# Output projection, both layer normalizations and the feed-forward part in one block

## The chip, the cores and the metric

The kernel runs on one core of one Trainium2 chip. The metric is the device time of one execution in microseconds; the time before is the median of three runs. A core has five instruction streams that run side by side and wait for each other by semaphores: TensorE (PE), VectorE (DVE), ScalarE (ACT), GpSimd (POOL) and SyncE (SP), which here only issues transfers.

## The reference, cut to what matters

Two layers of a decoder trunk over 1040 tokens (16 learned ones ahead of 1024), width 1024. Each layer mixes tokens in two branches, projects, normalizes, runs a gated feed-forward part with a causal convolution of width 3, and normalizes again.

```python
h = _layer_norm(concat(meta, x), ln_in_g, ln_in_b)
for l in range(DEPTH):                       # DEPTH = 2
    p = h @ w_in[l]
    ...                                      # two branches, gates -> mixed
    h = _layer_norm(DEEPNORM_ALPHA * h + mixed @ w_out[l], ln1_g[l], ln1_b[l])
    f = _conv_ffn(h, w_up[l], conv_w[l], conv_b[l], w_down[l])
    h = _layer_norm(DEEPNORM_ALPHA * h + f, ln2_g[l], ln2_b[l])
return h[:, N_META:]
```

`_layer_norm` takes mean and variance over the 1024 channels of a token: `(x - mu) * rsqrt(var + 1e-5) * g + b`. Everything is float32.

## The kernel before, in words

**Layout.** Activations lie transposed: channels on the 128 partitions, tokens along the free dimension (TP = 1044, in NB = 3 pieces of 348). The stream `h` is eight tiles (KD = 8) of 128 x 1044. For precision each operand of a large product is split into a high part, which fp32r holds, and the low rest (`h_hi`, `h_lo`; `w_hi`, `w_lo`), and `product` (lines 187 to 197) sums three passes, hi x hi, lo x hi and hi x lo: for a 128-column unit of weights 8 x 3 x 3 = 72 matmuls into one of two groups of three PSUM banks (`pset[0]`, `pset[1]`).

**Weights.** Each unit of weights takes one of two slots: SP loads it into `w_raw` (`load_unit`), GpSimd makes `w_hi` and `w_lo` from it (`split_unit`, lines 225 and 227), TensorE uses it. A slot of `w_raw` is free again when it is split, a slot of `w_hi` and `w_lo` when its product is done.

**Phases.** `Phase` opens a block with its own semaphores and programs for the engines, and ends in a barrier over all engines (line 121), after which no engine has work in flight. The two layers are one hardware loop over `layer(l)`. Around the change the phases are:

- The opening (lines 285 to 416): loads the tokens, normalizes them by token in three groups of chunks, transposes them, and makes `h_hi` (ScalarE) and `h_lo` (GpSimd, line 393) through four staging buffers. It also collects the per-channel vectors and stores them to DRAM at its end.
- The input projection's first phase (lines 497 to 614): five units of `w_in` are loaded, split and multiplied; ScalarE begins with issuing twelve transfers of other weights and tables.
- The output projection (lines 2027 to 2065): eight units of `w_out`; VectorE reads each product out as `r` (ALPHA * h_hi + product) and `l` (+ ALPHA * h_lo) into `acc`, eight float32 tiles.
- `layer_norm` (lines 2070 to 2119), a phase of its own. TensorE multiplies a matrix of ones with all eight tiles of `acc` for the mean (24 fp32 matmuls, two records each); VectorE subtracts it (`c0` to `c7`); ScalarE squares, TensorE sums the squares in the same way; ScalarE makes the reciprocal root (`ln`, `rs`); then for each tile VectorE scales (`n`), ScalarE adds the bias and writes `h_hi` (`hi`), VectorE writes `h_lo` (`lo`), and only then starts the next tile:

```python
for k in range(KD):
    dves.did(stt(acc[:, k, :], acc[:, k, :], vecs[:, g_col + k:g_col + k + 1], lrs[:, :], ALU.mult, ALU.mult), f"n{k}")
    low(k)
```

- The feed-forward part (lines 2148 to 2360): the 22 channel tiles are taken in 11 groups of two, alternately called A and B. Four up products of a group, then eight down products of the group before it, whose results VectorE adds to `acc` (`d0` to `d7`, line 2314). ScalarE and VectorE do the convolution, the SiLU and the gating between. At its start ScalarE and VectorE rebuild `acc` = ALPHA * (h_hi + h_lo) (lines 2261 and 2302).
- `layer_norm` again, then the next layer, or `final_output`, which adds `h_hi` and `h_lo` (line 431), transposes and stores.

The order on each engine is written out by hand; every named step adds one to its engine's semaphore, and others wait for that count.

Of the kernel before, what the change touches and what calls it, by code (L numbers as in the profile page):

```python
# [15 lines left out]
F32 = mybir.dt.float32  # L16
# [108 lines left out]
def build(nc, a, out):  # L125
# [61 lines left out]
    def product(bank, kt, lhs_hi, lhs_lo, rhs_hi, rhs_lo):  # L187

        last = None
        for k in range(kt):  # L190
            passes = ((lhs_hi, rhs_hi), (lhs_hi, rhs_lo), (lhs_lo, rhs_hi))
# [59 lines left out]

    cursor[0] = base
# [21 lines left out]
    for g, chunks in enumerate(in_groups):  # L274
# [6 lines left out]
        for k in range(KD):  # L281
            act_names += [f"aff{g}_{k}", f"hi{g}_{k}"]
            pool_names.append(f"lo{g}_{k}")
    dve_names += [f"row{n}_{i}" for n in range(DEPTH) for i in range(3)]
    with Phase(nc, "const_loaded", "inv_loaded", "act_steps", "dve_steps", "pool_steps", "pe_tr", "pe_rows", "rows_loaded", "vecs_out",
               *[f"tok{i}_loaded" for i in range(NC)]) as (block, sm):
        const_loaded, inv_loaded, act_s, dve_s, pool_s, pe_tr, pe_rows, rows_loaded, vecs_out = sm[0:9]
        tok_loaded = sm[9:]
# [4 lines left out]
        def _(sp):  # L293
# [93 lines left out]
        def _(pool):  # L387
            pools.give(pool)
            for g, chunks in enumerate(in_groups):
                c0, n = chunks[0], len(chunks)  # L390
                for k in range(KD):
                    pool.wait_ge(acts.sem, acts.of(0, f"hi{g}_{k}"))
                    pools.did(nc.gpsimd.tensor_tensor(h_lo[:, k, c0 * CH:(c0 + n) * CH], hst[(g * KD + k) % 4][:, 0:n * CH],
                                                      h_hi[:, k, c0 * CH:(c0 + n) * CH], ALU.subtract), f"lo{g}_{k}")

# [71 lines left out]
    def layer(l):  # L467
# [29 lines left out]
        with Phase(nc, "raw0_loaded", "raw1_loaded", "hi_done", "split", "used", "act_steps", "dve_steps", "pe_tile",  # L497
# [13 lines left out]
            totals = [1, 1, 2, 2, 2 + len(mix)]  # L511

            @block.sync
            def _(sp):
                split.give(sp)
                for u in range(5):
                    load_unit(sp, u, u % 2, loaded, split, units[u])
                    if u == 1:
                        sp.dma_start(vecs[:, :], vecs_d[l]).then_inc(vecs_in, 16)
# [6 lines left out]
            def _(pool):  # L526
                used.give(pool)
                for u in range(5):
# [1497 lines left out]
        acc = place("acc", [P, KD, TP], F32, TOP)  # L2026
        with Phase(nc, "raw0_loaded", "raw1_loaded", "hi_done", "split", "used", "dve_steps") as (block, sm):
            loaded, hi_done, split, used = stream(sm[0:5])
            dves = Steps(sm[5], ["r0", "l0", "r1", "l1"])
            w_out_v = a["w_out"][l].rearrange("(k p) n -> p k n", p=P)  # L2030

            @block.sync
            def _(sp):
                split.give(sp)
                with sp.Fori(0, KD // 2) as i:
                    for s in range(2):
                        load_unit(sp, i * 2 + s, s, loaded, split, [(kview(KD), w_out_v[:, :, ds(i * (2 * P) + s * P, P)])])

            @block.gpsimd
            def _(pool):  # L2040
                used.give(pool)
                with pool.Fori(0, KD // 2) as i:
                    for s in range(2):
                        split_unit(pool, i * 2 + s, s, i + 1, loaded, hi_done, split, (used.sem, used.of(i * 2 + (s - 1))))

            @block.tensor
            def _(pe):
                with pe.Fori(0, KD // 2) as i:
                    for s in range(2):
                        pe.wait_ge(split.sem, split.of(i * 2 + (s + 1)))  # L2050
                        pe.wait_ge(dves.sem, dves.of(i, f"r{s}", 1))
                        product(pset[s], KD, wtile(w_hi[s], KD), wtile(w_lo[s], KD), hk(m_hi), hk(m_lo)).then_inc(used.sem, 1)

            @block.vector
            def _(dve):
                dves.give(dve)
                stt = nc.vector.scalar_tensor_tensor
                with dve.Fori(0, KD // 2) as i:
                    for s in range(2):
                        def at(tile):  # L2060
                            return tile[:, ds(i * 2 + s, 1), :].rearrange("p o t -> p (o t)")
                        dve.wait_ge(used.sem, used.of(i * 2 + (s + 1)))
                        dves.did(stt(chunks3(at(acc)), chunks3(at(h_hi)), ALPHA, pset[s], ALU.mult, ALU.add), f"r{s}")
                        dve.wait_ge(dves.sem, dves.of(i, f"r{s}"))
                        dves.did(stt(at(acc), at(h_lo), ALPHA, at(acc), ALU.mult, ALU.add), f"l{s}")

        def layer_norm(g_col, b_col):  # L2070
            cursor[0] = base
            sq2 = [after(f"ln_sq{i}", [P, TP]) for i in range(2)]
            lrs = after("ln_rs", [P, TP])
            with Phase(nc, "pe_steps", "act_steps", "dve_steps") as (block, sm):
                pes = Steps(sm[0], ["mean"] + [f"v{k}" for k in range(KD)])
                acts = Steps(sm[1], [f"sq{k}" for k in range(KD)] + ["ln", "rs"] + [f"hi{k}" for k in range(KD)])
                dves = Steps(sm[2], [f"c{k}" for k in range(KD)] + [f"{n}{k}" for k in range(KD) for n in ("n", "lo")])

                @block.tensor
                def _(pe):  # L2080
                    pes.did(product32(pset[0], [(ones[:, :], acc[:, k, :]) for k in range(KD)]), "mean")
                    for k in range(KD):
                        pe.wait_ge(acts.sem, acts.of(0, f"sq{k}"))
                        for n in range(NB):
                            last = nc.tensor.matmul(pset[1][:, n, :], ones[:, :], sq2[k % 2][:, nrange(n)], start=(k == 0), stop=(k == KD - 1))
                        pes.did(last, f"v{k}")

                @block.scalar
                def _(act):
                    acts.give(act)  # L2090
                    for k in range(KD):
                        act.wait_ge(dves.sem, dves.of(0, f"c{k}"))
                        if k >= 2:
                            act.wait_ge(pes.sem, pes.of(0, f"v{k - 2}"))
                        acts.did(nc.scalar.activation(sq2[k % 2][:, :], acc[:, k, :], ACT.Square), f"sq{k}")
                    act.wait_ge(pes.sem, pes.of(0, f"v{KD - 1}"))
                    acts.did(nc.scalar.activation(chunks3(lrs[:, :]), pset[1], ACT.Ln, bias=EPS_LN, scale=1.0 / DM), "ln")
                    act.wait_ge(acts.sem, acts.of(0, "ln"))
                    acts.did(nc.scalar.activation(lrs[:, :], lrs[:, :], ACT.Exp, scale=-0.5), "rs")
# [316 lines left out]
```

## Time and profile before

| | us |
|---|---|
| median of 3 runs | 4536.91 (4532.87 to 4538.57) |
| the profiled execution | 4534.88 |
| its span, first to last instruction | 4533.1 |
| mean granted clock of TensorE, share of full | 0.932 |
| TensorE busy | 3877.1 (86%) |
| VectorE busy | 2027.8 (45%) |
| ScalarE busy | 1066.1 (24%) |
| GpSimd busy | 936.5 (21%) |

Busy times are sums over the span; engines overlap. In the rows further down a time at the start of a line is counted from the span's first instruction, the second number is the duration, and the bracket at the end says how long the engine had been idle and what released it.

### The profile page before, as it was taken

To read this page: it belongs to the slowest core of one execution; us is meant where nothing else is said; L and a number is where in the kernel's file an instruction comes from. 1 tells how busy PE (TensorE), PEld (TensorE's weight loads), DVE (VectorE), ACT (ScalarE), POOL (GpSimd) and SP (SyncE) were. 2 spreads that over 40 slices of the span, in tenths; PEclk is the share of its full clock that TensorE was granted. 3 is DMA by queue.
4 is the path that set the end of the run, shared out by engine and by line. 5 is a ranking of instruction groups with operands and counts; after the bars stand their busy time and mean duration, and the time that the engine had idled before them with its cause. 6 is when DMAs were issued, how large, how long until landed. Compare 5 with 4: busy or idle time off the path is not lost. (4 is left out here: it accounts for less than half of the span.)

```text
span 4533.1 us, 68171 instructions
## 1 busy us (share of the span) xinstructions
PE 3877.1 (86%) x28391; PEld 3522.9 (78%) x28391; DVE 2027.8 (45%) x2448; ACT 1066.1 (24%) x1504; POOL 936.5 (21%) x464
## 2 busy tenths in 40 slices
PE   3978889898795899999868889898968679999995
PEld 3655888886685899999754569797858579999993
DVE  2145346564415454454422434575633354445454
ACT  3245124222103111121222531341210121212112
POOL 3000320000231333333110014000013133333330
PEclk9988999999898999999978889998988889999997
DMA  4221236421310111111024112553222011111110
GB/s 100 70 68 29 80 110 188 121 70 59 112 32 28 43 47 43 47 47 43 14 63 105 48 34 84 162 163 85 65 98 80 5 47 47 43 47 43 47 38 37
DMA packets 370423, 305.20 MB, mean 67 GB/s; under 512 B 118167, under 2 KB 323571, under 8 KB 370147
## 3 DMA queue, kind: packets, MB, share of 16 engines
q1 hardware_dynamic: 331588, 243.02, 19.0%
q10 hardware_dynamic: 38559, 58.12, 3.7%
q8 instruction: 220, 3.60, 0.3%
q14 instruction: 56, 0.46, 0.0%
HBM read 218.82 MB, written 82.26 MB: 66 GB/s over the span
## 5 line engine op out<-in xcount | busy, mean ns | idle before, releaser
L225 POOL TENSOR_TENSOR w_hi<-w_raw,consts 128x1024 fp32r<-128x1024 f32 (+1 forms) x218 | 392.9, 1802 | 3410.7 <-PE psum L194 1226.1
L194 PE MATMUL psum<-h_hi,w_hi 128*128 128x348 f32 x3792 | 822.7, 326 | 222.1 <-POOL w_lo L227 182.2
L194 PEld LDWEIGHTS psum<-h_hi,w_hi 128*128 128x128 f32 x3792 | 644.9, 190 | 231.3 <-POOL w_lo L227 184.5
L194 PE MATMUL psum<-h_lo,w_hi 128*128 128x348 f32 x3792 | 813.8, 323 | 0.0
L194 PE MATMUL psum<-h_hi,w_lo 128*128 128x348 f32 x3792 | 811.2, 322 | 0.0
L194 PEld LDWEIGHTS psum<-h_lo,w_hi 128*128 128x128 f32 x3792 | 647.4, 190 | 0.0
L194 PEld LDWEIGHTS psum<-h_hi,w_lo 128*128 128x128 f32 x3792 | 642.0, 189 | 0.0
L227 POOL TENSOR_TENSOR w_lo<-w_raw,w_hi 128x1024 fp32r<-128x1024 f32 (+1 forms) x218 | 521.8, 2393 | 17.1
L2314 DVE TENSOR_TENSOR acc<-acc,psum 128x1044 f32<-128x1044 f32 x176 | 217.8, 1238 | 160.2 <-PE psum L194 157.0
L2332 DVE SCALAR_TENSOR_TENSOR cv_g<-up_g,cw,cv_g 128x1044 f32<-128x1044 f32 x44 | 137.7, 3130 | 336.7 <-ACT cv_g L2278 336.7
L2332 DVE SCALAR_TENSOR_TENSOR cv_v<-up_v,cw,cv_v 128x1044 f32<-128x1044 f32 x44 | 146.8, 3336 | 302.3 <-ACT cv_v L2278 302.3
L194 PE MATMUL psum<-f_hi,w_hi 128*128 128x348 f32 x1056 | 227.9, 324 | 21.3 <-DVE acc L2314 20.8
L839 PE MATMUL psum<-kh,qh 96*116 96x512 f32 (+6 forms) x480 | 192.4, 520 | 40.2 <-DMA kh<-k_scratch 24.3
L194 PE MATMUL psum<-f_lo,w_hi 128*128 128x348 f32 x1056 | 225.5, 322 | 0.0
L194 PE MATMUL psum<-f_hi,w_lo 128*128 128x348 f32 x1056 | 223.8, 320 | 0.0
L194 PEld LDWEIGHTS psum<-f_hi,w_hi 128*128 128x128 f32 x1056 | 177.1, 188 | 27.5 <-DVE acc L2314 26.5
L194 PEld LDWEIGHTS psum<-f_hi,w_lo 128*128 128x128 f32 x1056 | 178.9, 188 | 0.0
L2275 ACT ACTIVATE up_g<-psum 128x1044 f32<-128x1044 f32 x44 | 46.0, 1046 | 559.8 <-PE psum L194 559.8
L194 PEld LDWEIGHTS psum<-f_lo,w_hi 128*128 128x128 f32 x1056 | 177.6, 188 | 0.0
L839 PEld LDWEIGHTS psum<-kh,qh 96*116 96x116 f32 (+1 forms) x480 | 86.5, 206 | 103.5 <-issue 59.3
L853 PE MATMUL psum<-ident,pr 116*116 116x116 f32 (+1 forms) x720 | 116.3, 297 | 33.8 <-ACT prt L922 29.8
L194 PE MATMUL psum<-y_hi,w_hi 128*128 128x348 f32 x384 | 86.0, 334 | 68.7 <-POOL w_lo L227 68.7
(260 smaller groups left out, 5276.8 us busy)
## 6 DMA issues: line engine op xcount, KB each, us to landing
w_raw<-in_w_up SPq DMA_DIRECT2D x88, 512.0 KB, 3.8
w_raw<-in_w_in SPq DMA_DIRECT2D x68, 512.0 KB, 5.1
w_raw<-in_w_down SPq DMA_DIRECT2D x44, 512.0 KB, 3.5
gate_scratch<-gst ACTq DMA_DIRECT2D x32, 522.0 KB, 3.0
gbuf<-gate_scratch SPq DMA_DIRECT2D x32, 522.0 KB, 3.6
prep_scratch<-prep ACTq DMA_DIRECT2D x8, 2080.0 KB, 8.2
pc<-prep_scratch SPq DMA_DIRECT2D x20, 832.0 KB, 4.5
rkv_scratch<-mixed_p ACTq DMA_DIRECT2D x24, 522.0 KB, 4.3
```

The source lines that it names most:

```text
L194: last = nc.tensor.matmul(bank[:, n, :], w(k), x(k)[:, nrange(n)], start=(k == 0 and q == 0), stop=(k == kt - 1 and q == 2))
L225: nc.gpsimd.tensor_tensor(w_hi[s][:, 0:width], w_raw[s][:, 0:width], consts[:, 4:5].broadcast_to([P, width]), ALU.mult).then_inc(hi_done.s ...
L227: nc.gpsimd.tensor_tensor(w_lo[s][:, 0:width], w_raw[s][:, 0:width], w_hi[s][:, 0:width], ALU.subtract).then_inc(split.sem, 1)
L839: last = nc.tensor.matmul(score_view(e, c, min(c + 512, n), width(i)), qh[g % 2][e][:, i * QB:end_of(i)], kh[g % 2][e][:, c:min(c + 512, n ...
L853: last = nc.tensor.transpose(psum[0:width(c), 6 + n % 2, (c % 4) * QB:(c % 4) * QB + width(i)], pr[e][0:width(i), c * QB:end_of(c)], ident ...
L2275: acts.did(nc.scalar.activation(up[x_, p_][:, 2:TP + 2].rearrange("p (b n) -> p b n", b=NB), pset[0 if x_ == "g" else 1], ACT.Copy), f"r{x ...
L2314: dves.did(nc.vector.tensor_tensor(chunks3(acc[:, m, :]), chunks3(acc[:, m, :]), pset[m % 2], ALU.add), f"d{B}{m}")
L2332: dves.did(stt(c[:, :], up[x_, p_][:, 1:TP + 1], w[:, 1, col, p_:p_ + 1], c[:, :], ALU.mult, ALU.add), f"t1{x_}{B}{p_}")
```

## The change

1. Output projection, first normalization, feed-forward part and second normalization become one phase with one set of semaphores, so three barriers in each layer go. The normalization's three programs are now functions (`norm_pe`, `norm_act`, `norm_dve`) that are called inside it.
2. The mean comes from one tile `tot`, the running sum of the eight tiles of `acc`. VectorE adds each tile as it becomes final (`t0` to `t7` in the output projection, `t1` to `t7` after the last accumulations), and TensorE multiplies the ones with `tot` alone: 3 matmuls for 24.
3. `norm_dve` issues `n(k+1)` ahead of the wait for `hi(k)`.
4. The first up product waits for `lo(k)` tile by tile (`tile_ready`), not for a barrier. Its weights are loaded as soon as the last two units of `w_out` are split. GpSimd splits the first after the seventh output product, and the second after the eighth and after `c0`.
5. ScalarE alone rebuilds the residual: in place, ALPHA * acc + ALPHA * bias, after `hi7`.
6. The first two units of the next layer's `w_in` are loaded once the last two down units are split; ScalarE makes `w_hi` after `dA3` and `dA7`, VectorE makes `w_lo` within the centring, after `c4` and `c6`. In the last layer this is done too, with layer one's weights, and isn't used. For layer one the opening does it: SP issues both loads behind those of the tokens, GpSimd splits them between its second and third group of `lo`. The input projection starts with both units in place and loads from the third on.

```diff
+            for u in range(2):
+                sp.dma_start(kview(KD)(w_raw[u]), first_unit(0, u)).then_inc(first_in, 16)
...
+                if g == 1:
+                    pool.wait_ge(first_in, 32)
+                    for u in range(2):
+                        pools.did(nc.gpsimd.tensor_tensor(w_hi[u][:, :], w_raw[u][:, :], consts[:, 4:5].broadcast_to([P, 1024]), ALU.mult), f"whi{u}")
+                        pool.wait_ge(pools.sem, pools.of(0, f"whi{u}"))
+                        pools.did(nc.gpsimd.tensor_tensor(w_lo[u][:, :], w_raw[u][:, :], w_hi[u][:, :], ALU.subtract), f"wlo{u}")
...
-                for u in range(5):
+                sp.sem_inc(split.sem, 2)
+                for u in range(2, 5):
                     load_unit(sp, u, u % 2, loaded, split, units[u])
...
+        def norm_pe(pe, n):
+            n.pe.did(product32(pset[0], [(ones[:, :], tot[:, :])]), "mean")
...
+        def norm_dve(dve, n, other=None):
...
+            for k in range(KD):
+                n.dve.did(stt(chunks3(acc[:, k, :]), pset[0], -1.0 / DM, chunks3(acc[:, k, :]), ALU.mult, ALU.add), f"c{k}")
+                if other is not None:
+                    other(k)
+            dve.wait_ge(n.act.sem, n.act.of(0, "rs"))
...
+            scaled(0)
+            for k in range(KD):
+                if k + 1 < KD:
+                    scaled(k + 1)
+                dve.wait_ge(n.act.sem, n.act.of(0, f"hi{k}"))
+                n.dve.did(stt(h_lo[:, k, :], acc[:, k, :], vecs[:, n.b_col + k:n.b_col + k + 1], h_hi[:, k, :], ALU.add, ALU.subtract), f"lo{k}")
...
                 for s in range(UP):
+                    if s < 2:
+                        pool.wait_ge(o_used.sem, o_used.of(KD - 1 + s))
+                    if s == 1:
+                        pool.wait_ge(n1.dve.sem, n1.dve.of(0, "c0"))
                     split_unit(pool, s, s % 2, s // 2 + 1, loaded, hi_done, split, free(-1, NU // 2 + s))
...
+                def tile_ready(k):
+                    pe.wait_ge(n1.dve.sem, n1.dve.of(0, f"lo{k}"))
...
+                for k in range(KD):
+                    act.wait_ge(n1.dve.sem, n1.dve.of(0, f"lo{k}"))
+                    n1.act.did(nc.scalar.activation(acc[:, k, :], acc[:, k, :], ACT.Identity, bias=ab[:, k:k + 1], scale=ALPHA), f"acc{k}")
...
+                for s in range(2):
+                    act.wait_ge(next_in[s], 16)
+                    act.wait_ge(pes.sem, pes.of(NP, f"dA{4 * s + 3}"))
+                    nc.scalar.activation(w_hi[s][:, :], w_raw[s][:, :], ACT.Copy).then_inc(next_hi, 1)
...
+                        outs.did(nc.vector.tensor_tensor(tot[:, :], tot[:, :], at(acc), ALU.add), f"t{s}")
...
+                dve.wait_ge(pads, 2 * FG)
+                dve.wait_ge(n1.act.sem, n1.act.of(0, f"acc{KD - 1}"))
...
+                    n2.dve.did(nc.vector.tensor_tensor(tot[:, :], acc[:, 0, :] if m == 1 else tot[:, :], acc[:, m, :], ALU.add), f"t{m}")
+
+                def next_split(k):
+                    if k in (4, 6):
+                        s = (k - 4) // 2
+                        dve.wait_ge(next_hi, s + 1)
+                        nc.vector.tensor_tensor(w_lo[s][:, :], w_raw[s][:, :], w_hi[s][:, :], ALU.subtract).then_inc(next_lo, 1)
+                norm_dve(dve, n2, next_split)
```

## Rows read from the trace of the kernel before

**Rows 1.** Busy PE, PEld, DVE, ACT, POOL by stretch; granted clock, DMA share, GB/s
```profile
1345.00:1427.00 82.00, 30.60 (x101) 19.15 (x99) 42.04 (x36) 30.48 (x28) 6.21 (x3) 0.73 0.05 13
73.00:89.00 16.00, 0.00 (x0) 0.00 (x0) 0.06 (x1) 0.00 (x0) 4.49 (x3) 1.00 0.74 178
```

**Rows 2.** Timeline of TensorE, first normalization and first up product
```profile
1349.11 3.44 PE L209 MATMUL psum<-acc,ones 128*128 128x348 f32 x6 [3.55 <-PEq L121]
...
1426.99 1.24 PE L194 MATMUL psum<-h_hi,w_hi 128*128 128x348 f32 x3 [45.41 <-POOL w_lo L227]
```

**Rows 3.** Timeline of VectorE, last output product and first normalization
```profile
1345.74 1.24 DVE L2063 SCALAR_TENSOR_TENSOR acc<-h_hi,psum 128x1044 f32 x1 [8.84 <-PE psum L194]
1347.10 1.25 DVE L2065 SCALAR_TENSOR_TENSOR acc<-h_lo,acc  x1
1364.87 9.31 DVE L2111 SCALAR_TENSOR_TENSOR acc<-psum,acc 128x1044 f32<-128x1044 f32 x8 [16.52 <-PE psum L209]
1385.17 1.30 DVE L2118 SCALAR_TENSOR_TENSOR acc<-acc,vecs,ln_rs 128x1044 f32<-128x1044 f32 x1 [10.99 <-ACT ln_rs L2099]
1387.70 1.30 DVE L2116 SCALAR_TENSOR_TENSOR h_lo<-acc,vecs,h_hi 128x1044 fp32r<-128x1044 f32 x1 [1.23 <-ACT h_hi L2102]
1388.93 1.30 DVE L2118 SCALAR_TENSOR_TENSOR acc<-acc,vecs,ln_rs 128x1044 f32<-128x1044 f32 x1
...
1413.99 1.30 DVE L2116 SCALAR_TENSOR_TENSOR h_lo<-acc,vecs,h_hi 128x1044 fp32r<-128x1044 f32 x1 [1.23 <-ACT h_hi L2102]
```

**Rows 4.** Timeline of ScalarE, start of the feed-forward part
```profile
1416.07 7.82 ACT L2261 ACTIVATE acc<-h_hi 128x1044 f32<-128x1044 f32 x8 [2.11 <-PEq L121]
1440.35 1.05 ACT L2275 ACTIVATE up_g<-psum 128x1044 f32<-128x1044 f32 x1 [16.47 <-PE psum L194]
...
1451.81 1.05 ACT L2275 ACTIVATE up_v<-psum 128x1044 f32<-128x1044 f32 x1 [9.30 <-PE psum L194]
```

**Rows 5.** Timeline of VectorE, start of the final output
```profile
4505.42 9.34 DVE L431 TENSOR_TENSOR hs<-h_hi,h_lo 128x1044 f32<-128x1044 f32 x8 [0.99 <-PEq L121]
```

**Rows 6.** Timeline of VectorE, second normalization of layer one
```profile
2219.05 1.24 DVE L2314 TENSOR_TENSOR acc<-acc,psum 128x1044 f32<-128x1044 f32 x1 [1.62 <-PE psum L194]
2237.08 9.31 DVE L2111 SCALAR_TENSOR_TENSOR acc<-psum,acc 128x1044 f32<-128x1044 f32 x8 [16.78 <-PE psum L209]
2259.05 1.31 DVE L2118 SCALAR_TENSOR_TENSOR acc<-acc,vecs,ln_rs 128x1044 f32<-128x1044 f32 x1 [12.67 <-ACT ln_rs L2099]
...
2293.98 0.06 DVE L599 MEMSET gd<- 128x1 f32 x1 [4.80 <-issue]
```

**Rows 7.** Timeline of TensorE and ScalarE, start of layer two
```profile
2303.03 1.24 PE L194 MATMUL psum<-h_hi,w_hi 128*128 128x348 f32 x3 [47.56 <-POOL w_lo L227]
...
2309.51 0.54 ACTq L569 DMA_DIRECT2D w_uv<-in_w_uv  x1
2316.88 1.05 ACT L574 ACTIVATE latent<-psum 128x1044 f32<-128x1044 f32 x1 [29.04 <-PE psum L194]
```

**Rows 8.** Timeline of GpSimd, VectorE and TensorE, opening and first input product
```profile
51.95 9.24 POOL L393 TENSOR_TENSOR h_lo<-hst,h_hi 128x416 fp32r<-128x416 f32 x8 [10.34 <-ACT h_hi L384]
...
63.21 1.53 DVE L341 TENSOR_SCALAR tok<-tok,aggr,rstd 104x1024 f32<-104x1024 f32 x2 [13.81 <-ACT rstd L375]
...
75.96 0.06 DVE L599 MEMSET gd<- 128x1 f32 x1 [4.64 <-PEq L121]
...
84.75 1.89 POOL L225 TENSOR_TENSOR w_hi<-w_raw,consts 128x1024 fp32r<-128x1024 f32 x1 [11.43 <-DMA w_raw<-in_w_in]
86.73 2.34 POOL L227 TENSOR_TENSOR w_lo<-w_raw,w_hi 128x1024 fp32r<-128x1024 f32 x1
...
89.12 1.24 PE L194 MATMUL psum<-h_hi,w_hi 128*128 128x348 f32 x3 [18.09 <-POOL w_lo L227]
```

**Rows 9.** Busy time and TensorE's clock in two thinly used stretches, columns as rows 1
```profile
20.00:40.00 20.00, 6.59 (x32) 5.31 (x32) 8.46 (x16) 11.96 (x21) 7.01 (x7) 1.00 0.40 75
640.00:660.00 20.00, 12.04 (x32) 8.40 (x33) 6.73 (x7) 7.22 (x7) 0.00 (x0) 0.52 0.66 217
```

More of the change, by code:

```diff
@@ L185, in nrange, with product @@
         return slice(n * NW, (n + 1) * NW)
-    def product(bank, kt, lhs_hi, lhs_lo, rhs_hi, rhs_lo):
+    def product(bank, kt, lhs_hi, lhs_lo, rhs_hi, rhs_lo, ready=None):
         last = None
         for k in range(kt):
+            if ready is not None:
+                ready(k)
             passes = ((lhs_hi, rhs_hi), (lhs_hi, rhs_lo), (lhs_lo, rhs_hi))
@@ L527, in _ @@
                 used.give(pool)
-                for u in range(5):
+                pool.sem_inc(hi_done.sem, 2)
+                for u in range(2, 5):
                     split_unit(pool, u, u % 2, totals[u], loaded, hi_done, split, (used.sem, used.of(u - 1)))
@@ L2021, in layer @@
         merge(1, "w_proj_mla")
[L2026 to L2065, printed above, removed]
@@ L2132, in layer, with __init__ @@
         cw = [after(f"cw{i}", [P, 4, 2, FG]) for i in range(2)]
+        tot = after("tot", [P, TP])
+        lrs = tot
+        lsq = [after(f"lsq{i}", [P, TP]) for i in range(2)]
+        ab = after("ab", [P, KD])
         assert cursor[0] <= TOP, (cursor[0], TOP)
+        acc = place("acc", [P, KD, TP], F32, TOP)
+        class Norm:
+            def __init__(self, sems, before, more, g_col, b_col):
+                self.pe = Steps(sems[0], ["mean"] + [f"v{k}" for k in range(KD)])
+                self.act = Steps(sems[1], [f"sq{k}" for k in range(KD)] + ["ln", "rs"] + [f"hi{k}" for k in range(KD)] + more)
+                self.dve = Steps(sems[2], before + [f"c{k}" for k in range(KD)] + ["n0"] + [f"{n}{k + (n == 'n')}" for k in range(KD - 1) for n in ("n", "lo")] + [f"lo{KD - 1}"])
+                self.g_col, self.b_col = g_col, b_col
@@ L2194, in _ @@
                     load_unit(sp, NP * NU + UP + s, s, loaded, split, [(kview(FG, 512), down_source(NG - 1, s))])
+                for s in range(2):
+                    sp.wait_ge(split.sem, split.of(NP * NU + UP + s + 1))
+                    sp.dma_start(kview(KD)(w_raw[s]), first_unit(l * -1 + (DEPTH - 1), s)).then_inc(next_in[s], 16)
             @block.gpsimd
@@ L2222, in up_products @@
                             pe.wait_ge(dves.sem, dves.of(i, f"dB{KD - 2 + s}", 1))
-                        pes.did(product(pset[s % 2], KD, wtile(w_hi[s % 2], KD), wtile(w_lo[s % 2], KD), hk(h_hi), hk(h_lo)), f"{x_}{B}{pair}")
+                        pes.did(product(pset[s % 2], KD, wtile(w_hi[s % 2], KD), wtile(w_lo[s % 2], KD), hk(h_hi), hk(h_lo),
+                                        tile_ready if isinstance(i, int) and s == 0 else None), f"{x_}{B}{pair}")
                 def down_products(i, B, u, last_up):
@@ L2292, in _ @@
                     up_tiles(i, "B")
+                for s in range(2):
+                    act.wait_ge(next_in[s], 16)
+                    act.wait_ge(pes.sem, pes.of(NP, f"dA{4 * s + 3}"))
+                    nc.scalar.activation(w_hi[s][:, :], w_raw[s][:, :], ACT.Copy).then_inc(next_hi, 1)
+                n2.act.give(act)
+                norm_act(act, n2)
             @block.vector
```

155 lines of the change are left out of this document (90 added, 65 removed).

## The prediction

> **What bounds the kernel now.** I read the granted clock and busy shares by stretch first, then the timelines of the engines around the four layer normalizations and around the first input projection, then the clock in thinly used stretches. TensorE sets the pace of this kernel wherever there is a matrix product; what the change touches are holes between products. The stretches show them [rows 1]: from the last output-projection product to the first up-projection product TensorE has 30.6 us of records in 82 us, and nearly all of those are the ones-matmuls of the normalization. In the 16 us ahead of layer one's first input product it has nothing. The hole between the last down product and the next layer's first input product is built like the first. The change alters no product. So each hole is worth what its chain of single waits is worth, and I add up four holes of two kinds (each kind once per layer) and one in the opening.
>
> **Hole 1, twice: output projection, first normalization, first up product.** Before: the last product is read out by `r7` and `l7` on VectorE (1345.74 and 1347.10), then come a barrier and 24 fp32 ones-matmuls for the mean, so that the first centring `c0` starts at 1364.87; `n0` follows at 1385.17; eight times n, hi, lo end at 1413.99 + 1.30 = 1415.29 [rows 3]; then a barrier, the load, and the split of the first weights, and the product starts at 1426.99 behind `w_lo` [rows 2]. It ends at 1440.35, when ScalarE starts to read it [rows 4].
> After, step by step:
> - Mean. One more VectorE add (`t7`) of two SBUF tiles stands behind `l7`. Eight such adds took 9.34 us back to back [rows 5], 1.17 each; a single one with its wait I put at 0.12 + 1.25, like `l7`. So `t7` ends at 1348.35 + 1.37 = 1349.72. The barrier that stood here goes, but it is worth little: the mean started at 1349.11 anyway. The mean is now 3 matmuls (6 records) instead of 24 (48). The first 6 records of the old mean took 3.44 us at half clock [rows 2]; TensorE has been idle just as long again, so I take 3.44, and as the other end half of it, 1.72. `c0` starts at 1349.79 + 3.44 + 0.05 = 1353.3, 11.6 us earlier.
> - `c0` to `n0` is the same work. It took 20.30 us in layer one's first normalization [rows 3] and 21.97 in the second (2237.08 to 2259.05) [rows 6], where the clock had dropped ahead of the squares. Now only 3.4 us of TensorE work stand ahead of the same gap, so I take the slower, 21.97; the other end is 20.3, and with a second such drop 23.7. `n0` is at 1375.3.
> - Apply loop. Before, each k waits through n, hi, lo: 3.75 us. Now n(k+1) fills the wait for hi(k). VectorE starts an instruction every 1.23 us when nothing holds it (1387.70 to 1388.93), the first lo can start 2.53 us after n0 [rows 3]; a k costs 2 x 1.23 = 2.46. `lo7` starts at n0 + 2.53 + 6 x 2.46 + 1.3 = n0 + 18.6 and ends at n0 + 19.9, against n0 + 30.1 before: 10.2 us less.
> - First product. Its weights are loaded during the last two output products and split while TensorE works or the centring runs; GpSimd's unit 1 waits for `c0` and has 22 us of cover. The product follows lo tile by tile: a product of 72 matmuls takes 11.46 at full clock (1440.35 to 1451.81 [rows 4]), a tile's nine 1.43, less than 2.46, so only the last tile's 1.43 and a write-back come after `lo7`: end at n0 + 21.4 = 1396.7. Before: 1440.35. **Gain 43.6 us**, made of mean 11.6, minus 1.7 for the clock, apply loop 10.2, and 23.5 for barrier, load, split and all but the last tile of the product.
> - What is late next: ScalarE rebuilds the residual tiles now after hi7 (end near n0 + 18.6), eight tiles that cost 7.82 us before [rows 4]; at 1.1 each they end at n0 + 27.7, so the first read-out is 6.3 us behind the product. The third product is the first to need that bank, at n0 + 21.4 + 11.4 = n0 + 32.8, and the read-out is through at n0 + 29.9. Cover 3 us, cost nothing; every us beyond that would count.
> - The adds `t0` to `t6` lie in the 11.4 us between two reads, of which r and l use under 3: nothing.
> Two layers: 87.2 us.
>
> **Hole 2: second normalization, then the next layer.** The last accumulation `d7` starts at 2219.05, `c0` at 2237.08 [rows 6]. The running adds for tiles 1 to 6 need 1.24 + 1.25 + waits in the 2.86 us between down products (1.24 + 1.62 [rows 6]): they fit, with 0.2 us to spare; if they did not, the excess would count seven times at most. New: 1.24 + 0.12 + 1.25 + 0.07 + 3.44 + 0.05 puts `c0` at 2225.2, `n0` at 2247.2, end of `lo7` at 2267.1 against 2289.2: 22.1 less. Two low-part subtractions for the next weights (1.2 us each, at k = 4 and 6) lengthen the centring from 9.3 to 11.8; the squares, each paced by three ones-matmuls (half of 3.44, 1.72 us), need c7 only about 13 us after c0. Nothing.
> Then VectorE needed 4.80 us from the end of `lo7` to its first instruction of the next layer [rows 6], and the product waited until 2303.03 for the load and the split of its weights; it ended at 2316.88 [rows 7]. Now the weights are there: start at 2267.1 + 4.8 = 2271.9, same 13.85 us (cold start), end 2285.7. **Gain 31.1 us.** ScalarE issues its weight loads until 0.54 us after 2309.51 [rows 7], 20.9 us after `lo7`: new 2288.0, 2.3 us after the product. But TensorE needs its square only before the third product, at 2297: hidden.
> In the last layer only the 22.1 us count; the output stage behind it is unchanged. **Gain 22.1 us.** The surplus load of w_in hides under it.
>
> **Hole 3: opening.** The first product stood until 89.12 behind load and split, though the phase had begun near 75.96 [rows 8]. Against that, GpSimd gets four instructions (4 weight splits, 1.9 and 2.34 us each [rows 8], 8.6 together) between its second and third group of lo tiles: 51.95 + 9.24 + 8.6 = 69.8. ScalarE is held from its fifth tile on, since the four staging buffers wait for lo. I expect the phase to end 2.0 us later, bounds 0 and 6: VectorE's two normalizing instructions at 63.21 fall beside the splits, and the 1.05 MB more in the queue is 5.9 us of transfer at the 178 GB/s of 73:89 [rows 1], nearly all of it beside work that doesn't wait. New start 77.9. **Gain 11.2 us.**
> By the Trainium skill (SBUF — State Buffer, "Who interferes with whom") a VectorE instruction in a two-port mode and a GpSimd instruction exclude each other for the whole instruction, and the later one fully blocks. By that each of those two VectorE instructions could stand up to one split, 4.7 us in all, which would make the gain 8.5; no row of before has the pair side by side.
>
> **Sum.** 87.2 + 31.1 + 22.1 + 11.2 = 151.6 us off the profiled execution's 4534.88 (span 4533.1 and 1.8 around it): 4383.3. The median shown is 2.0 above that execution, so 4385.
>
> **The rivals.**
> - A, the clock stays at half through the product that is fed tile by tile, 0.13. For it: TensorE idles 9 us ahead of it and then works 1.43 of 2.46 us; at 640:660 it was busy 12.04 of 20 us and got 0.52 [rows 9]. Against it: at half clock a tile takes 2.86 us, more than the feed, so TensorE is busy without a break, and the product of 1426.99 lost only 13.36 - 11.46 = 1.9 us to a cold start, so it had its clock back after about 3.8 us [rows 2, 4]; and 20:40 got 1.00 with 6.59 busy [rows 9]. Price: 3.9 + 8 x 2.86 = 26.8 instead of 21.4, 5.4 twice, and the read-out slips by the same: 4385 + 11 = 4396. The Trainium skill (TensorE: Matmul & The Clock Gate, "A second HAM failure mode: psum-queue depth-cycling") says that frequent small idles between groups can make the clock swing; by it the cost would be the same 11 us, or less.
> - B, most of the warm-up goes, 0.07: mean and squares at full clock, 1.7 + 1.7 in each of four: 4371.
> - C, the gain in the holes is given back behind them, 0.07: the read-out of hole 1 misses its 3 us of cover, ScalarE's loads their 9, the opening ends 6 us late. 15 to 40 us: about 4412. Against it: all three covers were computed from measured spacing.
> - D, slower than before, 0.02: the clock, once half after the fed product, stays so in the feed-forward part. The point from which it decides: 151.6 us are lost again when 151.6 / 11.4 = 13 of the two layers' product equivalents run at half. With 20 it would be 4385 + 228 = 4613. Against: after every hole of before the clock came back.
> - E, the split weights or the running sum don't reach the path (a barrier or another load ends last), no change, 0.01: 4537.
>
> **How the numbers follow.** Forecast 0.70, own range 4376 to 4395 (mean and squares between their ends, opening 0 to 6 late). A and B lie on both sides. 4368 to 4408 leaves out D, E, most of C. A change under 0.2% (9 us) is what this measurement can't tell from none. Faster 0.97, same 0.01, slower 0.02.
>
> **What would show it.** Mean of 6 records, `c0` 7.5 us after the start of `r7`; lo starts 2.46 us apart; up product ending 51 us after `r7`; next layer's product 4.8 us after `lo7`; opening product at 78. Wrong if the third up product waits for ScalarE, if the clock in the fed product is 0.5, or if the opening phase ends after 80.

## Result and profile after

The changed kernel takes 4412.45 us (median of 4 runs, 4409.73 to 4415.18), the kernel before beside it 4537.63 (4532.87 to 4538.57). The ratio is 0.9729, with a 95% interval of 0.9714 to 0.9743. That is 2.7% faster; 4385 was forecast, and the time lies outside the range given, 4368 to 4408.

The span fell by 123.7 us (4533.1 to 4409.4) where the sum had 151.6, so 27.9 are missing. The page's first section, after:

```profile
span 4409.4 us, 67765 instructions
PE 3831.5 (87%) x28223; PEld 3493.3 (79%) x28223; DVE 2064.8 (47%) x2468; ACT 1072.4 (24%) x1510; POOL 925.7 (21%) x460
```

I measured each of the four normalizations in both traces by the same five marks: the start of the last read-out (`r7`, or `d7` in the second normalization), `c0`, `n0`, the end of `lo7`, and ScalarE's first reading of the product that follows. LN0 and LN2 are hole 1 in layers one and two, LN1 is hole 2, LN3 the last one. Microseconds, before -> after:

| | to `c0` | `c0` to `n0` | `n0` to end of `lo7` | `lo7` to the read | sum | gain | forecast |
|---|---|---|---|---|---|---|---|
| LN0 | 19.13 -> 7.95 | 20.30 -> 21.81 | 30.12 -> 22.08 | 25.06 -> 12.20 | 94.61 -> 64.04 | 30.6 | 43.6 |
| LN1 | 18.03 -> 5.55 | 21.97 -> 23.17 | 30.13 -> 19.77 | 27.70 -> 22.38 | 97.83 -> 70.87 | 27.0 | 31.1 |
| LN2 | 19.30 -> 7.95 | 20.30 -> 22.98 | 30.12 -> 22.08 | 24.52 -> 12.79 | 94.24 -> 65.80 | 28.4 | 43.6 |
| LN3 | 18.02 -> 4.64 | 21.98 -> 20.30 | 30.12 -> 19.78 | 12.40 -> 12.52 | 82.52 -> 57.24 | 25.3 | 22.1 |

The opening's first input product was done at 102.48 before and is done at 93.17 now (the time at which GpSimd, which waits for its end, goes on): 9.3 instead of 11.2. The five places give 120.6, and 3.1 came from elsewhere. That 3.1 is a net of larger terms: from the opening to LN0 the changed kernel's trace takes 4.4 us longer than the trace before, and from LN1 to LN2 5.9 us less (1237.8 for 1243.8, where every other trace of this case has 1242.0 to 1244.9). Single executions differ by several us in stretches that the change hardly touches. The miss sits in LN0 and LN2: 28.2 us, as much as the whole.

The busy table of the first hole and of the opening (columns as in rows 1, whose rows these answer to) shows a full clock in the opening and a mean of 0.71 of it in the hole, with 20.30 us of records on TensorE:

```profile
1340.00:1391.00 51.00, 20.30 (x59) 12.04 (x57) 33.48 (x26) 22.40 (x20) 9.31 (x4) 0.71 0.07 21
62.00:78.00 16.00, 5.45 (x22) 3.74 (x22) 6.58 (x8) 7.97 (x19) 13.61 (x12) 1.00 0.05 16
```

VectorE in LN0, after (start, duration, engine, line, operation, and in brackets the idle time ahead and what ended it). These rows answer to [rows 3]:

```profile
1340.81 1.24 DVE L2328 SCALAR_TENSOR_TENSOR acc<-h_hi,psum 128x1044 f32 x1 [7.55 <-PE psum L196]
1342.30 1.25 DVE L2330 SCALAR_TENSOR_TENSOR acc<-h_lo,acc  x1 [0.24 <-DVE acc L2328]
1343.58 1.25 DVE L2332 TENSOR_TENSOR tot<-tot,acc 128x1044 f32<-128x1044 f32 x1
1348.76 9.31 DVE L2093 SCALAR_TENSOR_TENSOR acc<-psum,acc 128x1044 f32<-128x1044 f32 x8 [3.94 <-PE psum L211]
1370.57 4.94 DVE L2099 SCALAR_TENSOR_TENSOR acc<-acc,vecs,tot 128x1044 f32<-128x1044 f32 x2 [12.49 <-ACT tot L2084]
1375.43 1.29 DVE L2105 SCALAR_TENSOR_TENSOR h_lo<-acc,vecs,h_hi 128x1044 fp32r<-128x1044 f32 x1
...
1377.86 1.29 DVE L2105 SCALAR_TENSOR_TENSOR h_lo<-acc,vecs,h_hi 128x1044 fp32r<-128x1044 f32 x1
...
1390.03 2.62 DVE L2105 SCALAR_TENSOR_TENSOR h_lo<-acc,vecs,h_hi 128x1044 fp32r<-128x1044 f32 x2
```

`c0` comes 7.95 us after `r7` (7.5 forecast), and the lo tiles start 2.43 apart (2.46 forecast). But `n0` and `n1` take 4.94 us together; in LN1 the same two take 2.52. TensorE in LN0, answering to [rows 2]:

```profile
1344.88 3.85 PE L211 MATMUL psum<-tot,ones 128*128 128x348 f32 x6 [4.24 <-DVE tot L2332]
1351.17 15.81 PE L2072 MATMUL psum<-lsq,ones 128*128 128x348 f32 x48 [2.44 <-ACT lsq L2080]
1391.47 1.21 PE L196 MATMUL psum<-h_hi,w_hi 128*128 128x348 f32 x3 [24.49 <-DVEq L2143]
```

The mean is 6 records. The up product doesn't start when `lo0` is there (1376.72), but 14.7 us later, beside `lo7`. What ended the wait is not a tile: DVEq is VectorE's sequencer, and line 2143 is the increment in `start_at`. The steps of the feed-forward part are counted by one semaphore for each engine, in rounds of a loop, and many waits ask for a step of the round before. Ahead of the first round (called iteration -1) nothing has been counted yet, so `start_at` adds a starting count once, as an instruction on that engine's own queue. ScalarE at the end of LN0, answering to [rows 4]:

```profile
1391.44 8.57 ACT L2277 ACTIVATE acc<-acc,ab 128x1044 f32<-128x1044 f32 x8
1404.85 1.05 ACT L2292 ACTIVATE up_g<-psum 128x1044 f32<-128x1044 f32 x1 [4.85 <-PE psum L196]
```

GpSimd in LN0:

```profile
1364.93 1.89 POOL L227 TENSOR_TENSOR w_hi<-w_raw,consts 128x1024 fp32r<-128x1024 f32 x1 [41.82 <-PEq L2143]
1366.90 2.34 POOL L229 TENSOR_TENSOR w_lo<-w_raw,w_hi 128x1024 fp32r<-128x1024 f32 x1
1369.20 1.90 POOL L227 TENSOR_TENSOR w_hi<-w_raw,consts 128x1024 fp32r<-128x1024 f32 x1
1371.17 3.23 POOL L229 TENSOR_TENSOR w_lo<-w_raw,w_hi 128x1024 fp32r<-128x1024 f32 x1
```

ScalarE's residual tiles are through at 1400.01 and wait for nothing; the product ends the wait at 1404.85. GpSimd's splits stood 41.82 us until the same line was reached on TensorE's queue, where it is behind the squares (their modelled end is 1366.98). So they run beside `n0` and `n1`, not beside the output product.

LN1 and the start of layer two, on TensorE, answering to [rows 7]:

```profile
2236.89 1.24 PE L196 MATMUL psum<-h_hi,w_hi 128*128 128x348 f32 x3 [28.21 <-SPq L532]
2237.93 0.49 PE L196 MATMUL psum<-h_lo,w_hi 128*128 128x348 f32 x1
2241.79 0.95 PE L196 MATMUL psum<-h_lo,w_hi 128*128 128x348 f32 x2 [3.36 <-issue]
```

The product starts 4.8 us after `lo7` (2232.04), as forecast, with its weights ready. Then there is a hole of 3.36 us after the fourth matmul, released by nothing that the trace knows.

The opening, answering to [rows 8], first VectorE's two normalizing instructions:

```profile
63.59 5.10 DVE L351 TENSOR_SCALAR tok<-tok,aggr,rstd 104x1024 f32<-104x1024 f32 x2 [13.82 <-ACT rstd L385]
```

GpSimd's four splits, in the same stretch:

```profile
61.53 1.89 POOL L408 TENSOR_TENSOR w_hi<-w_raw,consts 128x1024 fp32r<-128x1024 f32 x1
63.50 2.34 POOL L410 TENSOR_TENSOR w_lo<-w_raw,w_hi 128x1024 fp32r<-128x1024 f32 x1
65.80 2.34 POOL L408 TENSOR_TENSOR w_hi<-w_raw,consts 128x1024 fp32r<-128x1024 f32 x1
68.22 2.68 POOL L410 TENSOR_TENSOR w_lo<-w_raw,w_hi 128x1024 fp32r<-128x1024 f32 x1
```

And TensorE's first input product, which starts 0.8 us later than forecast:

```profile
78.69 1.24 PE L196 MATMUL psum<-h_hi,w_hi 128*128 128x348 f32 x3 [4.37 <-SPq L532]
```

### The profile page after: what moved, and what is told of

The parts are those of the page before. It is cut to its first block and busy times, and to the rows that moved or that the text cites. A ratio compares the mean times of both kernels' runs of the same rounds, so it can differ in the third digit from the quotient of the medians.

```text
span 4409.4 us, 67765 instructions
## 1 busy us (share of the span) xinstructions
PE 3831.5 (87%) x28223; PEld 3493.3 (79%) x28223; DVE 2064.8 (47%) x2468; ACT 1072.4 (24%) x1510; POOL 925.7 (21%) x460
## 5 line engine op out<-in xcount | busy, mean ns | idle before, releaser
L227 POOL TENSOR_TENSOR w_hi<-w_raw,consts 128x1024 fp32r<-128x1024 f32 (+1 forms) x214 | 381.0, 1780 | 3329.1 <-PE psum L196 1360.2
L1092 DVE TENSOR_TENSOR diff<-raw_p 128x1044 f32<-128x1044 f32 x28 | 50.2, 1793 | 209.8 <-ACT raw_p L1079 151.1
```

The source lines that it names most:

```text
L227: nc.gpsimd.tensor_tensor(w_hi[s][:, 0:width], w_raw[s][:, 0:width], consts[:, 4:5].broadcast_to([P, width]), ALU.mult).then_inc(hi_done.s ...
L1092: me.did(nc.vector.tensor_tensor(d[rows, :], raw[rows, 0:TP], raw[rows, 1:TP + 1], ALU.subtract), names[0])
```

## Experiments

All are edits of the changed kernel. Each has 4 runs beside runs of the kernel before on the same chip; where two experiments are compared over chips, it is by their ratios, and 0.001 is 4.5 us.

**1. VectorE's starting count ahead of the normalization.** The first up product waits for `dves` at iteration -1, which is satisfied by the increment alone. The increment stood on VectorE's queue behind all of `norm_dve`, so it came after `lo7`.

```diff
+start_at(dves, dve, "cwB")
 n1.dve.give(dve)
 norm_dve(dve, n1)
-start_at(dves, dve, "cwB")
```

> The changed kernel with one line moved: VectorE gives its step semaphore the starting count of the feed-forward part before norm_dve, not after it. Theory T1 (TensorE's first up product did not wait for lo(k) tile by tile, but for that starting count, which VectorE gives only when it has passed lo7): the first up product now starts with lo0 and ends 1.5 to 2 us after lo7 ends, instead of 12.3 us after it; each layer 10 to 11 us shorter, in all 20 to 22 us faster than the changed kernel's 4412 (4390 to 4392). Rival A of the prediction (clock at half through the fed product): the product starts with lo0, but ends some 6 us after lo7, gain 8 to 12 us. Rival R2 (something else holds the product, its weights or the bank): start stays at lo6, no change, 4412.

4391.9 us, ratio 0.9682 (0.9666 to 0.9698): 0.0047 less than the changed kernel, 21 us. The product now follows the tiles (TensorE, LN0):

```profile
1373.46 1.21 PE L196 MATMUL psum<-h_hi,w_hi 128*128 128x348 f32 x3 [9.89 <-DVE h_lo L2105]
...
1387.97 0.74 PE L196 MATMUL psum<-h_hi,w_hi 128*128 128x348 f32 x3 [0.74 <-DVE h_lo L2105]
```

GpSimd, which waits for the end of this product:

```profile
1391.24 1.90 POOL L227 TENSOR_TENSOR w_hi<-w_raw,consts 128x1024 fp32r<-128x1024 f32 x1 [20.24 <-PE psum L196]
```

The matmuls of the fifth, sixth and seventh tile each wait 0.72 to 0.74 us for their `h_lo`, and GpSimd is released at 1391.24, 2.0 after `lo7`, where the product ended 12.3 after `lo7` in the changed kernel. ScalarE reads at `lo7` + 7.27 instead of + 12.20, after its residual tiles. So about half of the gain shows in the marks of the table; the other half shows behind the read (from LN0's read to the last read-out ahead of LN1 773.7 us instead of 778.7, and from LN2's 773.3 instead of 777.7), because TensorE is already at the next product by then. The starting count was the failed step.

**2. TensorE's starting count ahead of the output product.** GpSimd's splits of the first up weights wait for `pes` in the same way.

```diff
+start_at(pes, pe, "gB0")
 with pe.Fori(0, KD // 2) as i:
...
 norm_pe(pe, n1)
-start_at(pes, pe, "gB0")
```

> The changed kernel with one line moved: TensorE gives its step semaphore its starting count before the output products, not after the normalization. Theory T2 (GpSimd's split of the first up weights waited for that count and so ran at 1365 to 1374, beside n0 and n1, two-input VectorE instructions, which took 4.94 us for two instead of 2.52): the splits run right after the seventh product and after c0, n0 and n1 take 2.5 us, lo7 ends 2.2 to 2.4 us earlier in each layer: 4 to 5 us faster than 4412. Rival: the slow n0 and n1 have another cause, they stay at 4.9 us and the time at 4412.

4412.83, 0.9728 (0.9712 to 0.9744): nothing. GpSimd now splits the unit behind `c0`, and VectorE's pair is back at its old price. GpSimd in LN0:

```profile
1344.72 1.89 POOL L227 TENSOR_TENSOR w_hi<-w_raw,consts 128x1024 fp32r<-128x1024 f32 x1 [15.60 <-DVE acc L2093]
```

VectorE in LN0:

```profile
1365.08 2.52 DVE L2099 SCALAR_TENSOR_TENSOR acc<-acc,vecs,tot 128x1044 f32<-128x1044 f32 x2 [12.44 <-ACT tot L2084]
```

`lo7` ends 19.77 after `n0` in LN0 and LN2, 2.3 less each, as expected. The product behind it starts cold and still waits for VectorE's count, and it gives part back: ScalarE reads at `lo7` + 13.26 and + 13.28 instead of + 12.20 and + 12.79. In the profiled execution the five places sum to 4.9 us less than in the changed kernel, and yet the span is the same. The rest took 5 us more, and most of that is the changed kernel's own trace: between LN1 and LN2 it is 7.1 us shorter than this one, and 4 to 7 us shorter than all others. The mechanism is shown, its price not by this run.

**3. Both.**

> Both moved lines. If T1 and T2 hold and add up: 24 to 27 us faster than the changed kernel, 4385 to 4388, and the first up product's read-out starts 51 to 52 us after r7 starts, as predicted, in place of 64. If the clock stays at half through the fed product: 4396 to 4400. If ScalarE's rebuilding of the residual tiles becomes late, the third up product shows idle time in front of it.

4383.82, 0.9670 (0.9654 to 0.9686): 8 us below experiment 1 by the medians (0.0012, 5 us, by the ratios), where twice 2.3 were expected; the intervals overlap. The forecast's 4385 was right for this kernel. The product ends (by GpSimd's release) 52.7 and 51.5 us after `r7`, as the forecast had it with 51; but its read-out starts at 58.0 and 56.8, not at the 51 to 52 expected here, because ScalarE's residual tiles are ahead of it. TensorE in LN0:

```profile
1372.32 1.07 PE L196 MATMUL psum<-h_lo,w_hi 128*128 128x348 f32 x3
...
1373.83 0.64 PE L196 MATMUL psum<-h_hi,w_hi 128*128 128x348 f32 x3
...
1383.21 0.75 PE L196 MATMUL psum<-h_hi,w_hi 128*128 128x348 f32 x3 [0.74 <-DVE h_lo L2105]
```

The product begins at 1368.70 and has its full clock from 1373.8 on (0.64 for three matmuls instead of 1.07). The busy table right behind, columns as in rows 1:

```profile
1383.00:1410.00 27.00, 26.79 (x168) 26.79 (x169) 11.48 (x13) 17.16 (x18) 8.61 (x4) 1.00 0.13 39
```

From the matmuls of the last two tiles on, TensorE works 26.79 of 27 us. It covers the start of the third product, which needs the bank that ScalarE reads late (1391.74, 7.26 after `lo7`). So that cover of 3 us held.

**4. The mean over eight tiles, without the running adds.**

```diff
-product32(pset[0], [(ones[:, :], tot[:, :])])
+product32(pset[0], [(ones[:, :], acc[:, k, :]) for k in range(KD)])
```

> The changed kernel with the running sum taken out: the mean is again 24 matmuls over the eight tiles. It prices the sum. My reckoning: 24 matmuls take 14 to 16 us instead of the 2.0 to 3.9 of three; the add that goes gives 1.3 back; the clock is then full at the mean's end, which saves 0 to 1.5 of the squares. 9.5 to 12 us in each of four normalizations: 38 to 48 us slower, 4450 to 4460. Rival: the mean is bound by something else (the read of c0, the semaphore chain), under 20 us slower.

4450.54, 0.9812 (0.9796 to 0.9829): the running sum is worth 0.0083, 38 us, in four normalizations. The old mean alone takes 17.3 us of TensorE, where 14 to 16 were expected. By the traces `c0` comes 12.1, 10.1, 10.8 and 11.0 us earlier with it, 44 together, and `c0` to `n0` is 5.4 longer (88.26 for 82.87): 38.6. TensorE in LN0:

```profile
1337.76 17.34 PE L211 MATMUL psum<-acc,ones 128*128 128x348 f32 x48 [2.84 <-DVE acc L2330]
```

**5. The old order n, hi, lo in the apply loop.** `scaled(k + 1)` ahead of the wait is taken out, and `scaled(k)` stands inside the loop again.

> The changed kernel with the apply loop in its old order (n, hi, lo of a tile, then the next tile). In the changed kernel the loop takes 19.8 us where no split runs beside it and 22.1 where the weights' splits do; in the kernel before it took 30.1. If the loop is bound by VectorE's waits as I reckoned, and the whole of it lies on the path of all four normalizations (TensorE starts behind lo6 or lo7 anyway): 8 to 10.3 us each, 35 to 41 us slower than the changed kernel, 4446 to 4454. Rival: part of the loop is covered by TensorE in the first normalization, 20 us slower or less.

4454.52, 0.9822 (0.9805 to 0.9838): the order is worth 0.0093, 42 us. In the trace `n0` to the end of `lo7` is 31.2, 30.1, 31.2 and 30.1 us, 39.0 more than in the changed kernel.

**6. No weights split ahead for the input projection.** The opening's and LN1's loads and splits are removed, and the projection loads and splits its first two units itself, as before the change.

> The changed kernel without the early load and split of the first two units of w_in: the input projection loads and splits all five units itself, the opening and the second normalization are as before in this. Theory: the opening's first product ends again near 102.4 instead of 93.2 (9 us), the one between the layers 22.9 us after VectorE enters the layer instead of 17.8 (5 us), together 14 us slower, 4424 to 4428. Rival (my prediction's sizes, 11.2 and 9.0): 20 us, 4432. In the profile TensorE's 3.36 us of 'issue' inside the first product of layer two should be gone, and lie under the wait for the weights.

4432.69, 0.9776 (0.9760 to 0.9792): worth 0.0047, 21 us. The opening's product is done at 104.16 (93.17), and LN1 takes 77.55 (70.87), 17.7 us in the two places together. The 14 us that were expected here were too few; the forecast's 20.2 fit the time better. LN1's product now waits for its weights and has no hole in it (TensorE):

```profile
2252.84 1.24 PE L196 MATMUL psum<-h_hi,w_hi 128*128 128x348 f32 x3 [40.10 <-POOL w_lo L229]
2253.88 1.07 PE L196 MATMUL psum<-h_lo,w_hi 128*128 128x348 f32 x3
```

**7. ScalarE's 12 weight transfers behind its first read.** It tests whether they cause the hole in LN1's product. They are issued after `latent_tile(0, 0, 0, 0)`.

> The changed kernel with ScalarE's twelve transfers of weights and tables issued after its first latent tile, not ahead of it. It asks where TensorE's 3.36 us of 'issue' after the fourth matmul of layer two's first product come from. Theory F1 (TensorE's instructions are fetched by DMA, and the fetch stands behind the bulk transfers that start at the same moment; the DMA share there is 1.0 and more): with the queues quieter the gap shrinks below 1.5 us and the product ends 2 to 3 us earlier. Theory F2 (the jump back to the loop's head costs this fetch whatever the transfers do): the gap stays at 3.0 to 3.7. The time: 4409 to 4413 either way, as long as the late loads stay hidden; if they don't, the end of the phase shows a wait for them.

4413.35, 0.9736 (0.9720 to 0.9752): no gain. The hole is 1.87 us (TensorE):

```profile
2230.09 0.95 PE L196 MATMUL psum<-h_lo,w_hi 128*128 128x348 f32 x2 [1.87 <-issue]
```

In the kernels that keep the transfers where they were it was 3.36, 1.76, 2.94, 1.64, 3.58, 1.53, 2.23 and 3.12 us (the changed kernel and experiments 1, 2, 4, 5, 3, 8 and 9), and 1.93 in the other one with late transfers (experiment 10). Both of these are 1.2 to 1.5 less than in the kernel that they are to be compared with, but they lie inside the spread of the others; neither theory's own figure came (under 1.5, or 3.0 to 3.7). So the transfers aren't shown to be the cause.

**8. TensorE kept busy, on top of experiment 3.** Matmuls whose results nobody uses are put ahead of the mean, between mean and squares, and behind the normalization.

```diff
+keep_warm(7, 5)
 pe.wait_ge(outs.sem, outs.of(KD // 2 - 1, "t1"))
...
 n.pe.did(product32(pset[0], [(ones[:, :], tot[:, :])]), "mean")
+keep_warm(7, 3)
...
 norm_pe(pe, n1)
+keep_warm(7, 12)
...
+keep_warm(7, 3)
 pe.wait_ge(n2.dve.sem, n2.dve.of(0, f"t{KD - 1}"))
 norm_pe(pe, n2)
+keep_warm(7, 30)
```

> The kernel with both starting counts given early, and TensorE kept busy with idle matmuls (results unused) in the gaps ahead of the mean, between mean and squares, ahead of the fed product and through the second normalization's apply loop. It asks what the half clock costs. Theory: with the clock at full the mean takes 2.0 instead of 3.9, c0 to n0 20.3 instead of 22 to 23, and the first product behind each normalization 11.5 to 12 instead of 13.4 to 13.9: 3.5 us in each of four and 2 in each of three, 15 to 20 us faster than 4384: 4364 to 4370. Rival: the idle matmuls themselves stand in front of the next needed one or the clock falls anyway, no gain or up to 5 us slower.

4376.0, 0.9653 (0.9637 to 0.9670): 0.0017, 8 us, below experiment 3, with intervals that overlap; 4364 to 4370 was expected, so half of the gain or more didn't come. The four normalizations of the profiled executions sum to 9.9 us less (230.96 for 240.84). TensorE in LN0:

```profile
1335.03 3.65 PE L204 MATMUL psum<-pair_mask,ident 104*104 104x416 f32 x10
1339.43 2.02 PE L211 MATMUL psum<-tot,ones 128*128 128x348 f32 x6 [0.75 <-DVE tot L2337]
1341.29 2.26 PE L204 MATMUL psum<-pair_mask,ident 104*104 104x416 f32 x6
```

The mean takes 2.02 instead of 3.85, and `c0` to `n0` is 20.30, 20.30, 20.31 and 20.30 us, against 21.81, 23.17, 22.98 and 20.30 in the changed kernel. The work in these stretches is the same in both kernels, and the granted clock over them was 0.87, 0.79, 0.80 and 1.00 in the changed kernel and 1.00 in all four here. So what the four differ by is the clock, and it is worth up to 2.9 us each. (Line numbers are shifted by the edits.)

**9 and 10. One unit of the input weights split ahead instead of two,** without the last `keep_warm`, on top of experiment 8; and the same with ScalarE's transfers late as in 7.

```diff
-for u in range(2):
+for u in range(1):
```

> Both starting counts early, idle matmuls ahead of the mean, the squares and the fed product (not through the second normalization's apply loop, where they brought nothing), and of the two units of w_in only the first is split ahead; the second is loaded ahead, and GpSimd splits it during the first product. Theory: in the opening GpSimd is free for the last lo group and VectorE's two normalizing instructions meet two splits instead of four, so the first product starts 1 to 3 us earlier than in the kernels with two; between the layers nothing changes. 4372 to 4375. Rival: the second unit's split comes late for the second product, which would show as a wait on w_lo ahead of it, 4376 or more.

> The same, and ScalarE's twelve transfers issued after its first latent tile. If the opening's and the second layer's first products were slowed by these transfers (a fetch of instructions behind them), up to 3 us less than its neighbour of this call. If not, the same within 3 us. The 'issue' gap in layer two's first product has been 1.5 to 3.6 us in eight kernels with the transfers in front, and 1.9 in the one with them behind.

4377.4, 0.9662 (0.9645 to 0.9679), and 4374.24, 0.9649 (0.9631 to 0.9666): neither can be told from experiment 8, and the 4372 to 4375 expected of the first was missed. With one split beside them, VectorE's two normalizing instructions take less, but no time follows from it (opening done at 91.64, against 91.07 in experiment 8). VectorE, opening, of experiment 9:

```profile
63.55 3.52 DVE L351 TENSOR_SCALAR tok<-tok,aggr,rstd 104x1024 f32<-104x1024 f32 x2 [13.81 <-ACT rstd L385]
```

So experiments 8 to 10 are the fastest kernels here, 3.4 to 3.5% under the kernel before.

## Why the prediction missed, step by step

**"The product follows lo tile by tile ... end at n0 + 21.4": the step that failed, 22.0 us.** The reasoning took the tiles as all that the product waits for. It also waits, at iteration -1, for the banks' earlier readers on VectorE. That condition is met from the start, but in this kernel "met" is an increment that VectorE itself issues, and it was queued behind the last `lo`. From `lo7` to the end of the product were 12.20 and 12.79 us instead of 1.5. Experiment 1 moved that one line, and 21 us came back.

**"GpSimd's unit 1 waits for `c0` and has 22 us of cover": failed in the same way, 4.4 us in the trace.** The increment on TensorE's queue came after the squares, so all four splits used up the cover and then fell beside `n0` and `n1` (4.94 instead of 2.52 us for the pair). Experiments 2 and 3 show the mechanism. Its price by time lies between 0 (experiment 2) and 5 to 8 us (3 against 1), and no run here can tell it from none.

**Mean: right.** `c0` at 7.95 for 7.5 in LN0 and LN2 (0.9 us of the miss in both), and at 5.55 and 4.64 for 6.2 in LN1 and LN3. In these two the mean kept some or all of its clock. Experiment 4 gives the size: 44 us of earlier `c0` less 5.4 of clock behind it, where the forecast had 47 (11.6 twice, 11.9 twice) less 3.4.

**Clock: the right size, and more spread.** 21.97 was taken for `c0` to `n0`; it came as 21.81, 23.17, 22.98 and 20.30. The ends given, 20.3 and 23.7, hold all four. The sum over four is 88.26 for 87.88: no part of the miss as a whole, though 0.9 too much in LN0 and LN2. Rival A, the fed product at half clock, can't be judged in the changed kernel, since nothing was fed. In experiment 3 it was: after some 5 us TensorE had its full clock and kept it through the waits of 0.74 us (granted 1.00 from 1373.83 to 1383.00, with 6.68 of 9.17 us busy). Rival A is wrong there. Rival B's warm-up (1.7 + 1.7 in each of four, 13.6) didn't go by itself; when it was driven out in experiment 8, the ratio fell by 0.0017 (8 us), with intervals that overlap, and the four normalizations of the traces by 9.9 us.

**Apply loop: right.** 19.77 after `n0` where GpSimd was still (19.9 forecast); experiment 5 puts the order at 42 us in four.

**Weights split ahead in LN1: right at the start, 3.7 us short behind it.** The wait for them went as forecast (product 4.8 after `lo7`), but a new stall of 3.36 us appeared in the product. It is hidden when the product waits for its weights (experiment 6). Nearly all of the remaining 0.4 is a slower cold start. The whole step, opening included, is worth 21 us by the time and 17.7 by the traces of the two places; 20.2 were forecast (9.0 and 11.2).

**LN3: 3.2 us better** than forecast, since the clock stayed (`c0` 1.5 earlier, 1.7 less to `n0`).

**Opening: 1.9 us short, inside the bounds.** The product started at 78.69 for 77.9, and its cold run was 14.5 for 13.4 us. The two normalizing instructions took 5.10 for 1.53, 3.6 more. The Trainium skill's rule (SBUF — State Buffer, "Who interferes with whom") says that such a pair excludes each other for a whole instruction, and the trace agrees in direction: 3.6 lies inside the 4.7 worked out beside it. The gain by that rule was 8.5, mine 11.2, and 9.3 lies between, nearer to the rule. With one split beside them they took 3.52 (experiment 9), as waiting for one GpSimd instruction would have it.

**ScalarE's residual tiles: cost nothing, as said.** The read-out behind them starts at `lo7` + 7.26, and no product waits (experiment 3). Rival C named a time, 4412, that is nearly the one measured, but its mechanism (gains given back behind the holes) isn't what happened: the covers held, and the loss lies inside holes 1. The account of the miss is 22.0 + 4.4 + 0.9 (mean) + 0.9 (`c0` to `n0`) in LN0 and LN2, 4.2 in LN1 (3.7 after `lo7`), and 1.9 in the opening, less 3.2 in LN3 and 3.1 elsewhere: 28.0 for 27.9. That it closes so well is partly luck, since the 3.1 is the net of larger terms in one execution, the 4.4 and 5.9 above among them; the 22.0 doesn't rest on it, because experiment 1 gave it back by time.

**Open.** What the 3.36 us in LN1's first product are. They vary from 1.5 to 3.6 us between kernels, come after the same fourth matmul, behind the jump back to the layer's start, and didn't exist before the change or in the opening. The traces speak for a late fetch of instructions, though no experiment was made on it. The profile has transfers of the kind "instruction"; on its queue q8 a packet of 16 KB lands 3.44 us after the start of this product in the changed kernel, and the fifth matmul starts 1.45 later. In all ten kernels with the hole such a packet lands 1.7 to 3.7 us after the product's start, and the fifth matmul follows 1.25 to 1.55 us behind it, however long the hole is. In the changed kernel three of these packets, counted from the product's start, land at -1.4, 3.4 and 10.0. In the kernel before and in experiment 6, where TensorE waits for its weights, three land at -10.5, -6.4 and 0.4 and at -13.3, -8.0 and -1.7, and no hole appears. The packet alone is not enough: one lands 2.2 us after the start of the opening's product too, which has no hole. Why it comes later in some kernels than in others stays open. And at the start of the feed-forward groups A, TensorE still waits 14.18 us for VectorE's counts, in both kernels and both layers; no experiment was made on it.

## What to carry to other kernels

When a wait is to be satisfied by a starting count, the count is work like any other: ask which queue issues it and what is ahead of it there. A product "follows its tiles" only if every other wait of it, those for the previous round included, is met earlier. When a split or cast on GpSimd is made free of one wait, look up at once which VectorE instructions it will run beside, and whether their operands lie in SBUF. And when the marks of one trace add up to a gain that the times don't show, compare the stretches that the change doesn't touch first: here such a stretch alone differed by 7 us between two traces.

## Hardware behaviour not expected

- GpSimd's splits slow some VectorE instructions to two or three times their length and others not at all. VectorE's `acc,vecs,tot` pair took 4.94 instead of 2.52 us, the opening's pair 5.10 instead of 1.53, and the running add of two SBUF tiles 3.33 instead of 1.25; the read-out with a PSUM operand just ahead of that add kept its 1.24, and so did the eight centring instructions, which also read PSUM (9.30 us beside splits in experiment 3, 9.31 without):

```profile
1306.51 1.24 DVE L2328 SCALAR_TENSOR_TENSOR acc<-h_hi,psum 128x1044 f32 x1 [5.14 <-PE psum L196]
...
1309.47 3.33 DVE L2332 TENSOR_TENSOR tot<-tot,acc 128x1044 f32<-128x1044 f32 x1
```

  Here the add is hidden: r, l and t need 6.3 of the 11.4 us between two products.
- Short idle stretches cost TensorE's clock differently each time: the same chain of squares and ones-matmuls put `n0` at `c0` + 20.30 to + 23.17 within one execution, at a granted clock of 1.00 to 0.79. Matmuls without use in the waits brought all four to 20.3, at a clock of 1.00.
